# Compression products of the sample phase: three per pair of blocks instead of four, and the output gate applied in prompt attention

## The reference

```python
sub = rows[:M * 16].reshape(M, 16, 2, 4, 64)              # M = 128 blocks for a sample
first  = jnp.einsum('mpchd,cpde->mche', sub, cmp_w1[:, :16])
second = jnp.einsum('mpchd,cpde->mche', sub, cmp_w1[:, 16:])
hid = jax.nn.silu(first[:-1] + second[1:] + cmp_b1[None, :, None, :])
out = jnp.einsum('mche,ced->mchd', hid, cmp_w2)           # then norm and rotation of the keys
```

## Time and profile before

| what | value |
|---|---|
| time, median of 3 runs | 2028.19 us (2023.22 to 2030.3) |
| profiled execution, its own time | 2025.66 us |
| its span, first to last instruction | 2023.9 us |
| PE busy | 1839.7 us, 91% |
| DVE busy | 735.2 us, 36% |
| ACT busy | 431.2 us, 21% |
| POOL busy | 186.0 us, 9% |
| mean granted TensorE clock | 0.949 |

### The profile page before, as it was taken

The page is one execution under the profiler, slowest core; times in us unless marked ns, Lnnn a source line. Parts: engine busy times, 40 slices in busy tenths (PEclk is TensorE's granted clock), DMA queues, the critical chain, the costliest instruction groups (busy, mean ns, idle before and its releaser), DMA issues. The chain is left out here.

```text
span 2023.9 us, 23652 instructions
## 1 busy us (share of the span) xinstructions
PE 1839.7 (91%) x9119; PEld 1087.3 (54%) x9119; DVE 735.2 (36%) x1614; ACT 431.2 (21%) x956; POOL 186.0 (9%) x294
## 2 busy tenths in 40 slices
PE   5779999999999999997998999859898999999778
PEld 3245646564655465555873447735554454454467
DVE  3212333323242323240102035027773655555332
ACT  1301211221121112110002011225462222223210
POOL 0000110010001000100000000024342111111000
PEclk8869999999999999998998999869899999999879
DMA  9941571255144513545121135540004355444521
GB/s 295 386 180 42 209 249 44 97 195 208 44 146 166 187 68 123 199 154 204 63 84 42 42 83 187 145 137 1 2 1 187 125 218 218 187 187 187 153 79 44
DMA packets 126329, 281.70 MB, mean 139 GB/s; under 512 B 33992, under 2 KB 46734, under 8 KB 119287
## 3 DMA queue, kind: packets, MB, share of 16 engines
q1 hardware_dynamic: 104588, 170.59, 25.2%
q0 software_dynamic: 16384, 109.54, 13.7%
q10 hardware_dynamic: 5268, 0.36, 0.3%
HBM read 227.81 MB, written 60.86 MB: 143 GB/s over the span
## 5 line engine op out<-in xcount | busy, mean ns | idle before, releaser
L1082 DVE SCALAR_TENSOR_TENSOR mlstm_cring<-mlstm_cring,mlstm_cur_old,mlstm_bank 128x512 f32<-128x512 f32 x128 | 87.1, 744 | 223.4 <-PE mlstm_bank L844 223.4
L1369 PE MATMUL proj_bank<-stage,area 128*128 128x512 f32 x320 | 143.0, 606 | 6.3 <-ACT area L1446 6.3
L1571 PE MATMUL sample_bank<-area 128*128 128x508 f32 x256 | 121.3, 610 | 7.2 <-DVE area L1565 7.2
L762 PE MATMUL mlstm_bank<-h,stage 128*128 128x272 f32 x512 | 120.4, 398 | 4.1 <-SPq L650 4.1
L817 PE MATMUL mlstm_bank<-h,stage 128*128 128x272 f32 x512 | 121.2, 395 | 0.0
L1571 PE MATMUL sample_bank<-sample_xt,area 128*128 128x508 f32 x256 | 114.8, 598 | 0.0
L828 PE MATMUL mlstm_bank<-stage,h 128*128 128x512 f32 x256 | 114.1, 599 | 0.0
L762 PEld LDWEIGHTS mlstm_bank<-h,stage 128*128 128x128 f32 x512 | 98.3, 193 | 25.2 <-SPq L650 4.2
L817 PEld LDWEIGHTS mlstm_bank<-h,stage 128*128 128x128 f32 x512 | 96.0, 190 | 27.9 <-issue 9.1
L779 PE MATMUL mlstm_bank<-stage,h 128*128 128x512 f32 x256 | 110.9, 594 | 0.0
L1369 PEld LDWEIGHTS proj_bank<-stage,area 128*128 128x128 f32 x320 | 61.1, 193 | 87.9 <-issue 86.3
(11 more groups left out here) (509 smaller groups left out, 2626.9 us busy)
## 6 DMA issues: line engine op xcount, KB each, us to landing
stage<-in_a_w_in SPq DMA_DIRECT2D x16, 2048.0 KB, 9.6
mlstm_cring<-in_state_C SPq DMA_DIRECT2D x32, 1024.0 KB, 5.5
o_Cs<-mlstm_cring POOLq DMA_DIRECT2D x32, 1024.0 KB, 4.8
stage<-in_a_ada_w SPq DMA_DIRECT2D x4, 2048.0 KB, 15.0
sample_winr<-in_cache_kv_win SPq DMA_DIRECT2D x8, 1024.0 KB, 5.4
o_win_s<-in_cache_kv_win SPq DMA_DIRECT2D x1, 8128.0 KB
stage<-in_w_kv SPq DMA_DIRECT2D x3, 2048.0 KB, 9.0
act_scratch<-mlstm_szt POOLq DMA_DIRECT2D x4, 1088.0 KB, 6.5
```

What stands on the lines that cost most here:

```text
L762: last = pe.matmul(o[:, 0:HALF], win[:, 0, k, i * P:(i + 1) * P], S.h[:, k, at:at + HALF], start=(k == 0), stop=(k == KD - 1))
L1082: dve.scalar_tensor_tensor(c, c, cur_old[:, n:n + 1], bank[:, b_big("outer", n * KH + k), :], ALU.mult, ALU.add).then_inc(E["c_new"], 1)
L1369: last = pe.matmul(o, h[:, k, a * P:(a + 1) * P], w[:, k, :], start=(k == 0), stop=(k == KD - 1))
L1571: last = pe.matmul(out, w1[:, c, o * 8 + k, :], xt[:, k // 2, :, k % 2, o:o + M - 1], start=(k == 0 and o == 0), stop=(k == 7 and o == 1))
```

## The change

With the blocks x, first-half weights A and second-half weights B, the first layer is A x[m] + B x[m+1]. For an even block 2j and the odd one after it the new form uses

- set 1: (A+B) x[2j+1], which both need
- set 2: B (x[2j+2] - x[2j+1]), for the odd one
- set 3: A (x[2j] - x[2j+1]), for the even one

Each set is 8 products of 256 columns. The weight sum `w12` is made once on POOL. The differences are made by POOL for every sample and c, in two subtractions: the first into a buffer `after` (one for c=0 and c=1), the second in place. The transposes on DVE sort even and odd blocks into two halves, for which the page numbers are loaded in another pattern. Set 1 goes to bank 3, ACT copies it to `hid`, sets 2 and 3 go to the two halves of bank 7, DVE adds the copy to both (`add_both`), and ACT applies SiLU. The second layer moves to bank 4 and waits for the sums of the sample before. `w12`, `after` and the samples' part of the gate lie in the space of `S.sz`, which is free because the prompt's gate is now multiplied in by POOL during prompt attention (`gated`).

```diff
@@ page numbers, SP and POOL in phase_prompt
-            four = I["page_table"].rearrange("n (t j) -> j n t", j=4)
+            eight = I["page_table"].rearrange("n (t j) -> j n t", j=8)
             for a in range(4):
-                for j in range(4):
-                    at = 32 * a + 8 * j
-                    sp.dma_start(S.quarters[at:at + 8, :, :], four[j].partition_broadcast(8),
+                for j in range(8):
+                    at = 32 * a + 4 * j
+                    sp.dma_start(S.quarters[at:at + 4, :, 0:4:2], eight[j].partition_broadcast(4),
...
+            pool.tensor_scalar(odd, even, float(PAGE // 4), C("quarter_of_page")[:, 1:2], ALU.mult, ALU.add)
+            pool.drain()
+            pool.tensor_scalar(even, even, float(PAGE // 4), C("quarter_of_page")[:, 0:1], ALU.mult, ALU.add)
@@ gate, POOL in phase_prompt
+            def gated(pr, g):
+                m = pr * G + g
+                pool.wait_ge(E["o_ok"], m + 1)
+                pool.tensor_tensor(S.ot[:, m, 0:TP], S.ot[:, m, 0:TP], S.sz[:, m, 0:TP], ALU.mult)
             for u in range(N):
+                if u - 6 in last_of_pair:
+                    gated(*last_of_pair[u - 6])
...
+            gated(*last_of_pair[N - 1])
+            pool.drain()
@@ POOL in phase_sample
+            def differences(m, c):
+                hold(pool, E["xt_ok"], m * 2 + c + 1, E["pass_pool"])
+                x = flat(xt[c], "pqhbm").rearrange("p (j o m) -> p j o m", o=2, m=M // 2)
+                d = flat(after, "pqhbj").rearrange("p (x j) -> p x j", j=M // 2)
+                pool.tensor_tensor(d[:, :, 0:M // 2 - 1], x[:, :, 0, 1:], x[:, :, 1, 0:M // 2 - 1], ALU.subtract)
+                pool.drain()
+                pool.tensor_tensor(x[:, :, 0, :], x[:, :, 0, :], x[:, :, 1, :], ALU.subtract)
+                pool.drain().then_inc(E["diff_ok"], 1)
...
+            for c in range(2):
+                pool.tensor_tensor(w12[:, c, :, :], S.w1[:, c, 0:8, :], S.w1[:, c, 8:16, :], ALU.add)
+            pool.memset(after[:, :, :, :, M // 2 - 1:M // 2], 0.0)
+            pool.drain().then_inc(E["sum_ready"], 1)
+            differences(0, 0)
             next_rows(1)
+            pool.wait_ge(E["after_mm"], 1)
+            differences(0, 1)
+            pool.wait_ge(E["rows_in"], 64)
+            pool.wait_ge(E["after_mm"], 2)
+            differences(1, 0)
             with pool.Fori(1, NS - 1) as n:
                 hold(pool, E["rows_in"], n * 64, E["pass_pool"])
                 next_rows(n + 1)
+                hold(pool, E["after_mm"], n * 2 + 1, E["pass_pool"])
+                differences(n, 1)
                 next_sel(n)
+                hold(pool, E["after_mm"], n * 2 + 2, E["pass_pool"])
+                differences(n + 1, 0)
@@ PE in phase_sample, products
+                    if kind == 0:
+                        t = pe.matmul(both, w12[:, c, k, :], xt[c][:, k // 2, :, k % 2, M // 2:M], start=(k == 0), stop=(k == 7))
...
+                    elif kind == 1:
+                        if k == 0 and c == 1:
+                            pe.wait_ge(E["hid_ok"], m * 2 + 1)
+                        if k == 0:
+                            pe.wait_ge(E["diff_ok"], m * 2 + c + 1)
+                        t = pe.matmul(out[:, 1], S.w1[:, c, 8 + k, :], after[:, k // 2, :, k % 2, :], start=(k == 0), stop=(k == 7))
...
+                    else:
+                        t = pe.matmul(out[:, 0], S.w1[:, c, k, :], xt[c][:, k // 2, :, k % 2, 0:M // 2], start=(k == 0), stop=(k == 7))
@@ PE in phase_sample, where they stand in attend(n): before -> after, in steps of c=0, then c=1
+                    if c == 0:
+                        fill_in(0, range(0, 8))      # between the key and value halves of the second layer
-                fill_in(0, [0])
-                fill_in(0, [1])
-                fill_in(0, [2, 3])
+                fill_in(0, range(8, 13))             # after the window scores
-                fill_in(0, [4])
+                fill_in(0, range(13, 15))            # after the compressed scores
-                fill_in(0, [5])
+                fill_in(0, range(15, 18))            # after the group product
-                fill_in(0, [6, 7])
+                fill_in(0, range(18, 24))            # after the second selection scores
-                fill_in(1, [0, 1])
+                fill_in(1, range(0, 6))
-                fill_in(1, [2, 3])
+                fill_in(1, range(6, 12))             # ahead of the products with the values
-                fill_in(1, [4, 5, 6, 7])
+                fill_in(1, range(12, 24))
@@ DVE in phase_sample
+            def add_both(m, c):
+                dve.wait_ge(E["hid_mm"], m * 2 + c + 1)
+                x = bank[:, 7, :].rearrange("p (o x) -> p o x", o=2)
+                dve.tensor_tensor(x, x, bc(flat(hid[:, c, :, :], "phm")[:, 0:BKV * M // 2], 1, 2), ALU.add).then_inc(E["add_ok"], 1)
...
+                if next_c1:
+                    queries(n + 1)                   # the four small query copies, before at the head of attend
+                    add_both(n + 1, 1)
...
+            add_both(0, 0)
+            add_both(0, 1)
             blocks_out(1, 0, (0, 1, 2, 3))
@@ phase_output
-            for k in range(KD):
-                dve.tensor_tensor(S.ot[:, k, :], S.ot[:, k, :], S.sz[:, k, :], ALU.mult).then_inc(E["prod"], 1)
+            dve.tensor_tensor(S.ot[:, :, TP:T], S.ot[:, :, TP:T], S.szs[:, :, :], ALU.mult).then_inc(E["prod"], 1)
```

More of the change, by code:

```diff
@@ L1565, in turn_blocks, with turn_half_blocks @@
     return dve.transpose(out, src)
+def turn_half_blocks(dve, tile, xt, c, t):
+    src = tile.rearrange("p (q x) -> p q x", q=4)[:, :, c * BKV * BD:(c + 1) * BKV * BD]
+    at = t % 2 * 64 + t // 2 * 32
+    out = flat(xt, "pqhbm").rearrange("p (j m) -> p j m", m=PAST // CST)[:, :, at:at + 32]
+    return dve.transpose(out, src)
 def compress_products(pe, w1, xt, c, k, out, M):
@@ L2106, in room, with products @@
                     pe.wait_ge(E["out_d"], out_d_at(m, f))
[L2108 to L2112, removed]
-                    t = compress_products(pe, S.w1, xt[c], c, k, out, M)
-                if ks[-1] == 7:
-                    t.then_inc(E["hid_mm"], 1)
+            def products(m, c, steps):
+                both = bank[:, 3, 0:BKV * M // 2].rearrange("p (h j) -> p h j", h=BKV)
+                out = bank[:, 7, :].rearrange("p (o h j) -> p o h j", o=2, h=BKV)
+                for step in steps:
+                    kind, k = step // 8, step % 8
+                    if kind == 0:
+                        if k == 0:
+                            pe.wait_ge(E["xt_ok"], m * 2 + c + 1)
+                        t = pe.matmul(both, w12[:, c, k, :], xt[c][:, k // 2, :, k % 2, M // 2:M], start=(k == 0), stop=(k == 7))
+                        if k == 7:
+                            t.then_inc(E["both_mm"], 1)
+                    elif kind == 1:
+                        if k == 0 and c == 1:
+                            pe.wait_ge(E["hid_ok"], m * 2 + 1)
+                        if k == 0:
+                            pe.wait_ge(E["diff_ok"], m * 2 + c + 1)
+                        t = pe.matmul(out[:, 1], S.w1[:, c, 8 + k, :], after[:, k // 2, :, k % 2, :], start=(k == 0), stop=(k == 7))
+                        if k == 7:
+                            t.then_inc(E["after_mm"], 1)
+                    else:
+                        if k == 0:
+                            pe.wait_ge(E["both_ok"], m * 2 + c + 1)
+                        t = pe.matmul(out[:, 0], S.w1[:, c, k, :], xt[c][:, k // 2, :, k % 2, 0:M // 2], start=(k == 0), stop=(k == 7))
+                        if k == 7:
+                            t.then_inc(E["hid_mm"], 1)
             def turn_keys(n, fills):
@@ L2240, in attend @@
                 t.then_inc(E["pv_mm"], 1)
-                fill_in(1, [4, 5, 6, 7])
-            products(0, 0, range(8))
-            products(0, 1, range(8))
+                fill_in(1, range(12, 24))
+            pe.wait_ge(E["sum_ready"], 1)
+            products(0, 0, range(24))
+            products(0, 1, range(24))
             with pe.Fori(0, NS - 1) as n:
@@ L2247, in _ @@
             attend(NS - 1, False)
-            hold(pe, E["o2_ok"], NS + 1, E["pass_pe"])
+            hold(pe, E["o2_ok"], NS + 2, E["pass_pe"])
             for n in range(NS):
@@ L2308, in _ @@
                 attend(n, True)
-                silu(n + 1, 0)
             silu(NS - 1, 1)
@@ L2338, in keys_out, with queries @@
                 dve.tensor_copy(out, src).then_inc(E["out_d"], 1)
-            def attend(n, next_c1, next_c0):
+            def queries(n):
                 for pr in range(2):
@@ L2449, in _ @@
             dve.sem_inc(E["out_d"], 1)
+            dve.sem_inc(E["o2_ok"], 1)
+            queries(0)
             for c in range(2):
                 for t in range(4):
-                    last = turn_blocks(dve, S.stage[:, t * QUARTER:(t + 1) * QUARTER], xt[c], c, M, t)
```

(3 more changed lines are left out.)

51 lines of the change are left out of this document (37 added, 14 removed).

## The result

| | before | after |
|---|---|---|
| median, us | 2026.17 (2023.22 to 2030.3, 4 runs) | 2074.03 (2070.22 to 2079.24, 4 runs) |
| profiled execution / span, us | 2025.66 / 2023.9 | 2071.27 / 2069.5 |
| PE, DVE, POOL busy, us | 1839.7, 735.2, 186.0 | 1808.9, 811.3, 345.6 |
| mean granted clock | 0.949 | 0.928 |

The change makes the kernel slower: 1.0241 of the time before (95% interval 1.0226 to 1.0256), 47.9 us by the medians and 45.6 by the two profiled spans. The forecast was 2160, in a range of 2065 to 2215. The side was right, the size was not.

What follows compares the result with a forecast made beforehand. TensorE's work bounds the loop before; the change was to replace it with a GpSimd–DVE chain. Sample phase +121.7, prompt +11.6 and output -0.8 sum to +132.5 us, forecast 2160, range 2065 to 2215.

Steps and rivals of the forecast that it cites:

- What it puts on GpSimd: Sample phase: two subtractions for each of 16 pairs, of 4032 and 4096 elements a partition, at 2.08 ns an element.
- D: Time of one pair of GpSimd subtractions: 17.6 us, with 7.4 as lower and 21.0 as upper case.
- T = 2D + 24.5: Looped pass: the forced chain of differences, products and DVE work takes 59.7 us against 47.1.
- rival 2: GpSimd's second input nearly free, D 7.4; TensorE and DVE's key chain set a 43.8 us pass; about 2018 us, chance 0.1.
- the start: Ahead of the loop: weight sums and first differences on GpSimd delay the first pass, shift +38.3 us.
- the prompt's terms: Prompt attention: page loads +9.7, one more drained operation +0.4 and the last gate multiplication +1.5, together +11.6 us.
- six periods: Six looped passes, each 12.6 us longer than before, +75.6 us.
- four drains and signals: Looped pass: 0.4 us in the chain for all four.
- The hold: DVE operations with two SBUF inputs wait until a running GpSimd operation ends; norm_rope's first is held through the second subtraction.
- rival 3: DVE's small SBUF-to-SBUF copies held too: second layer some 3.4 us later a pass, +24, about 2184 us; chance 0.15.
- The page loads: Start of prompt attention: SP's sixteen loads become 32 of 64 elements, 26.5 us together, +9.7 on the path.
- The gate's tail: End of prompt attention: the eighth gate multiplication on GpSimd ends the phase, +1.5 us.

Runs made afterwards that it cites:

- experiment 2: Kernel after, the two drains in `differences` replaced by signals; 2072.43 us, 1.023 of before.
- experiment 6: Kernel after with its drains kept, only the query copies moved to where DVE waits for ACT's factors; 2077.0 us.
- experiment 7: Kernel before with only the gate's part: 2025.93 us; then also two unread GpSimd subtractions in every looped pass: 2029.28 us.
- experiment 5: Kernel after, signals for the drains in `differences` and behind the weight sums, query copies moved to DVE's wait for ACT's factors; 2030.68 us, ratio 1.0024.
- the other eight: Eight follow-up runs whose traces execute the same prompt code as after; the rest of prompt attention there cost up to +5.7 us.
- the freed pass: Kernel after with signals for those drains, query copies moved and all subtractions on VectorE; 2015.19 us, passes of 45.5 us after the first.

## Why the prediction was right on the side and wrong in size

**The step that failed is "What it puts on GpSimd": 4032 and 4096 elements a partition.** They are 2016 and 2048: `xt` has 4096 elements a partition in all, and a subtraction writes one for each pair of blocks. The rate was near: 2.08 ns an element taken, 2.2 measured. With half the elements D is 9.0 us, not 17.6; a subtraction under 5 us is what the prediction itself said would overturn it. The Trainium skill (GPSIMD Engine Reference, 3.1 Elementwise — side-by-side cycle accounting) gives 4497 ns for 2048 elements; the trace agrees with 4520 and 4530, and with 2292 for the same operation on VectorE, where the page has 2293.

**What the rest of the working would have said.** With D = 9.0 the formula T = 2D + 24.5 gives 42.5, under the 47.1 before, so that rival 2's TensorE and key chain would have set the pass at 43.8 (seven times -3.3); the start would come to 38.3 - 3*8.6 = +12.5. With the prompt's terms that sums to about no change. So the right side was luck: a factor of two stood in for two costs that the formula lacked. Measured at the prediction's own points (1580.00 before, the end of differences(1,0) at 1597.19 after, each from its phase's start at 1537.51 and 1526.93), the start lost 27.8 us where 38.3 was forecast, six periods 28.1 (51.8 us each) where 75.6 was, the last of the seven passes gained 5.0 where a loss of 7.8 was, and the eighth, put at 0, lost the 5.9 above.

**The drains.** Priced at 0.4 us a pass as "four drains and signals". Between the two subtractions alone GpSimd stood 51.0 us for six pairs of c=0 and 18.8 for seven of c=1. At the start, the corrected +12.5 plus the 8.8 us for which GpSimd stood behind the sums' drain and the 4.9 inside sample 0's pair of c=1 comes to 26.2, near the 27.8 measured.

**The hold.** Read rightly from one overlap of 0.34 us, and its victims only in part. norm_rope's first operation is held (L1160 took 694 ns on average in after, 426 before), but rival 3's mechanism, against which the prediction set "nothing in the trace shows a copy held", is the one that binds once the drains are gone: the query copies. Its place was right and its price of 3.4 us a pass was near the 4.9 us wait of experiment 2. In after itself it hid behind the drains (experiment 6). The Trainium skill (SBUF — State Buffer, Who interferes with whom) lists copies among the VectorE instructions that can contend with GpSimd for the shared port pair; experiment 7 agrees, with 8.89 us for four copies in one pass.

**Clock.** As forecast, the granted clock fell behind the long waits (0.91 in the loop against 1.00); it rose to 0.95 when the waits went (experiment 5).

**Prompt and output.** The page loads were priced at 0.83 us each from a line through two points of different layout; they took 0.37 (11.84 us for 32). +9.7 was forecast within bounds of 0 and +16.8, and TensorE's wait fell by 7.05. The gate's tail (+1.5) was near what this execution shows (+1.8) and low against the other eight (up to +5.7; +2.4 with the gate's part alone). The output (-0.8) was near: -0.6 from its first product on, -1.3 from the phase's start.

Not settled: why the freed pass stops at 45.5 us and not at rival 2's 43.8. TensorE's waits there are short ones on DVE and ACT, and none was taken away by itself.

## What to carry to other kernels

Count the elements of one instruction from its access pattern before you price it. On GpSimd, order dependent instructions by a signal, not by a drain, wherever a gather may be in flight; a gap "<-issue" behind a drain is the sign to look for in the old trace. Where GpSimd computes beside VectorE, keep VectorE's SBUF-to-SBUF instructions, small ones too, out of the front of anything that another engine waits for, and test two suspected waits together as well as one by one: here each alone was worth 1.6 us or less, and both with the drain of the sums 43.

## What the runs showed that was not expected

- A drain on GpSimd lasted until the gather ahead of it had landed: 14.73 us from issue, with 14.7 as the gather's median to landing.
- Four VectorE copies of 0.7 us together took 8.89 us beside two GpSimd subtractions, and the loop was not longer for it. DVE's transposes, some of which ran beside subtractions in after, kept their lengths (1219 and 1213 ns in after, 1219 and 1214 before), and so did the copies out of PSUM that did (0.38 us for 128x256).
- Loads of page numbers from SP cost by the element: 1088, 546 and 323 ns for 256, 128 and 64.
